# RWKV core: SyncE issues the next pair's vectors ahead of the scatter of the inverses

## What is computed

```python
def step(s, inp):
    r_t, w_t, k_t, v_t, a_t, b_t = inp
    sa = jnp.einsum('dbhvk,dbhk->dbhv', s, a_t)
    s = s * w_t[..., None, :] + sa[..., :, None] * b_t[..., None, :] + v_t[..., :, None] * k_t[..., None, :]
    return s, jnp.einsum('dbhvk,dbhk->dbhv', s, r_t)
```

## Time and profile before

| | |
|---|---|
| median of 3 runs | 3182.29 us (3176.93 to 3184.63) |
| profiled execution | 3185.66 us |
| its span | 3183.8 us |
| TensorE busy | 2941.7 us (92%) |
| VectorE busy | 1476.0 us (46%) |
| ScalarE busy | 684.6 us (22%) |
| GpSimd busy | 1123.4 us (35%) |
| granted clock of TensorE | 0.959 of full speed |

### The profile page before, as it was taken

The page is one execution under the profiler, slowest core; times in us unless marked ns, Lnnn a source line. Parts: engine busy times, 40 slices in busy tenths (PEclk is TensorE's granted clock), DMA queues, the critical chain, the costliest instruction groups (busy, mean ns, idle before and its releaser), DMA issues.

```text
span 3183.8 us, 59340 instructions
## 1 busy us (share of the span) xinstructions
PE 2941.7 (92%) x24772; PEld 2417.9 (76%) x24772; DVE 1476.0 (46%) x1845; ACT 684.6 (22%) x1013; POOL 1123.4 (35%) x663
## 2 busy tenths in 40 slices
PE   6799998899998489988998999999999999999996
PEld 0577886687776488988786888888888888888885
DVE  0676677445866434444425533333333343333336
ACT  0222222102222112122113212122222212122221
POOL 0343343434332112110343444444444444444442
PEclk7899998899999799999999999999999999999998
DMA  9675566532333654444432232232232233223332
GB/s 404 236 242 179 193 221 214 175 83 74 142 110 137 171 112 89 89 94 122 179 99 66 93 96 96 93 96 96 93 96 97 93 97 95 93 95 98 94 95 110
DMA packets 221753, 410.74 MB, mean 129 GB/s; under 512 B 133696, under 2 KB 135488, under 8 KB 214720
## 3 DMA queue, kind: packets, MB, share of 16 engines
q1 hardware_dynamic: 190880, 308.18, 30.9%
q10 hardware_dynamic: 30336, 96.64, 8.8%
q0 software_dynamic: 288, 2.10, 0.2%
HBM read 365.96 MB, written 40.91 MB: 128 GB/s over the span
## 4 chain that ended last, share of the span: by engine, by line
PE 62%; DVE 2%; issue 2%; DMA 0%; ACT 0%; POOL 0%; POOLq 0%; SPq 0%; DVEq 0%; ACTq 0%
PE bank L1075 17%; PE bank L1076 16%; PE bank L1074 16%; PE bank L797 7%; PE bank L813 2%; PE bank L885 1%; PE bank L873 1%; PE bank L959 1%; PE bank L957 1%; DVE buf L1941 0%; DVE buf L1942 0%; PE bank L821 0%; DMA buf<-lnrows 0%; PE bank L834 0%; DVE buf L1898 0%
## 5 line engine op out<-in xcount | busy, mean ns | idle before, releaser
L640 POOL TENSOR_TENSOR buf<-buf 128x1024 fp32r<-128x1024 f32 x288 | 696.6, 2419 | 1023.7 <-ACT buf L1274 1023.7
L1075 PE MATMUL bank<-buf 128*128 128x512 f32 x2304 | 911.2, 395 | 0.0
L1076 PE MATMUL bank<-buf 128*128 128x512 f32 x2304 | 907.4, 394 | 0.0
L1074 PE MATMUL bank<-buf 128*128 128x512 f32 x2304 | 901.3, 391 | 0.6 <-POOL buf L640 0.4
L1274 ACT CAST buf<-buf 128x1024 fp32r<-128x1024 f32 x288 | 302.6, 1051 | 1260.8 <-PE bank L1076 1259.5
L1074 PEld LDWEIGHTS bank<-buf 128*128 128x128 f32 x2304 | 433.1, 188 | 107.1 <-issue 3.2
L1075 PEld LDWEIGHTS bank<-buf 128*128 128x128 f32 x2304 | 432.6, 188 | 100.1 <-issue 0.5
L1076 PEld LDWEIGHTS bank<-buf 128*128 128x128 f32 x2304 | 432.4, 188 | 92.7
L664 PE MATMUL bank<-buf 128*128 128x512 f32 (+1 forms) x1168 | 430.1, 368 | 22.2 <-POOL buf L613 13.0
L665 PE MATMUL bank<-buf 128*128 128x512 f32 (+1 forms) x1168 | 422.6, 362 | 0.0
L666 PE MATMUL bank<-buf 128*128 128x512 f32 (+1 forms) x1168 | 417.1, 357 | 0.0
(11 more groups left out here) (219 smaller groups left out, 2200.6 us busy)
## 6 DMA issues: line engine op xcount, KB each, us to landing
buf<-stream SPq DMA_DIRECT2D x382, 512.0 KB, 3.5
buf<-adarows ACTq DMA_DIRECT2D x108, 512.0 KB, 4.9
buf<-ada SPq DMA_DIRECT2D x32, 1024.0 KB, 13.3
scaled_keys<-buf ACTq DMA_DIRECT2D x18, 768.0 KB, 5.5
buf<-scaled_keys SPq DMA_DIRECT2D x18, 768.0 KB, 6.6
buf<-adarows SPq DMA_DIRECT2D x20, 512.0 KB, 6.5
buf<-inverse_image SPq DMA_DIRECT2D x48, 192.0 KB, 5.2
buf<-tokens SPq DMA_DIRECT2D x4, 1536.0 KB, 21.5
```

Source lines behind the costliest of these rows:

```text
L640: G.tensor_tensor(wl2[b % SPLIT2], raw2[b], wh2[b % SPLIT2].bitcast(F32), ALU.subtract).then_inc(split2, 1)
L1074: pe.matmul(bank[:, :], lh, rh, start=start, stop=False)
L1075: pe.matmul(bank[:, :], lh, rl, start=False, stop=False)
L1076: return pe.matmul(bank[:, :], ll, rh, start=False, stop=stop)
```

## The change

In the loop over pairs 1 to 5, the call that loads the next pair's vectors moves from behind the scatter to ahead of it. No operation, transfer or wait is added or removed. In pairs 1 to 4 the scatter's four issues, and the waits in front of them, now stand behind the wait of the vectors' loads and their four issues; in pair 5 there are no vectors to load.

```diff
             load_receptances(1)
             for j in range(1, BPAIRS):
                 gather(j)
-                scatter(j)
                 if j + 1 < BPAIRS:
                     load_vectors(j + 1)
+                scatter(j)
                 load_inverses(j)
                 if j + 1 < BPAIRS:
                     load_receptances(j + 1)
```

## The result

The changed kernel takes 3199.21 us (median of 20 runs, 3185.0 to 3203.85) against 3182.86 us of the kernel before beside it (20 runs): ratio 1.0048, 95% interval 1.0038 to 1.0057, 16.3 us slower. Its profiled execution took 3199.28 us with a span of 3197.4 us.

A forecast was written before the change was run, and what follows sets the result against it. TensorE was taken to bound the kernel, the change acting through when it leaves the RWKV core. Arrival 9.2, clock 6.3 and later transfers 1.0 summed to +16.5 us: 3182.3 to 3199 us, range 3183 to 3213 (forecast case 3189 to 3212).

The forecast's parts named there:

- The vectors gain nothing: SyncE's queue: the next pair's vector loads wait for their buffers, not the scatter, so issuing them first gains 0.
- V: Time SyncE issues the vectors of pair j+1; claimed set by ScalarE's last front copy and unmoved by the change.
- The arrival of the inverses: Pairs 1 to 4: inverse loads wait for the scatter's landing behind the vectors, delaying TensorE's inverse; +9.2 us (+7.2 to +20).
- the high end of 15.6: Upper bound, in us after the vectors' issue, for the scatter's image being written; 14.8 was taken, low end 14.5.
- TensorE's clock and what follows: TensorE's clock falls after its wait at the inverse, +6.3 us; SyncE's later transfers cause pauses, +1.0 us.
- three longer falls: TensorE at half clock after the wait in three pairs of four, 3 x 2.1 = +6.3 us (0 to +9).
- The 1 us for receptances and late inputs: These loads, issued some 6 us later, run beside TensorE's inverse and bring pauses, 0.25 us a pair, +1 us.
- Cover and pass-through: The gather's substitution ends 17 us and more before the vectors' issue, covering its delay; the core's delay reaches the end in full.
- Side by side: Rival: scatter transfers beside the vectors, not behind them, so inverses land earlier; -14 us, 3168 us, chance 0.08.
- Arrival without the clock: Rival: TensorE arrives shortly before the inverses and its clock holds; +7 us, 3189 us, chance 0.16.
- That nothing happens: Rival: order changes but the wait for the image ends before the inverses matter; 0 us, 3182 us, chance 0.04.
- TensorE's mid-block pauses: Pauses such as 4.02 and 2.93 us before the inverse, at no program wait, during dense DMA traffic; instruction refills left unproved.

The follow-up runs named there:

- e1: Changed kernel without the scatter's four stores in pairs 1 to 4 and without the wait for their landing; 3181.60 us, ratio 1.0003 to the kernel before.
- e8: Order of the kernel before, but SyncE also waits for VectorE's last rc copy of the pair before, between vectors and inverses; 3197.65 us, ratio 1.0053.
- e5: Changed kernel with 60 spare matmuls on TensorE ahead of the wait for the inverses in pairs 1 to 4; 3195.39 us, ratio 1.0033.
- e2: Changed kernel with the scatter of pairs 1 to 4 stored to spare tensors, inverses loaded without waiting for its landing; 3190.01 us, ratio 1.0031.
- e4: Changed kernel reordered: scatter and inverses issued ahead of the next pair's vectors; 3173.61 us against 3180.53 of the kernel before, ratio 0.9982.
- e6: Changed kernel with K and V of the next pair issued behind the inverses, only A and B ahead of the scatter; 3195.10 us, ratio 1.0030.
- e7: Changed kernel reordered, inverses ahead of the next pair's A and B, its K and V only behind the next gather; 3185.78 us, ratio 1.0010.

## Why the prediction was right, point by point

**The time.** Forecast +16.5 us and 3199; measured 16.3 us and 3199.2. The sum is better than its terms: one was too small and another too large by nearly the same; that it fits to 0.2 us is luck.

**The vectors gain nothing.** Right: V follows F by 0.02 us in both kernels, and e1 has the time of before.

**The arrival of the inverses: forecast +9.2 us, measured +12.5.** The mechanism is shown (e1 takes it away, e8 makes it again by another way). Its size was low. The image was awaited until V+14.8, 14.8, 16.4 and 14.7, forecast 14.8; from first inverse load to TensorE's start it took 11.5, 12.5, 11.5 and 12.3 us, forecast 11.5 from the single case of pair 0. Pair 3's late image and two slow loads are the 3.3 us. The loads lie inside the bounds given, and so does the start of each inverse (V+26.3 to V+28.0 in 25.8 to 29.0), but pair 3's image at V+16.4 lies beyond the high end of 15.6; its second store alone took 5.2 us to issue.

**TensorE's clock and what follows: forecast +7.3 us, measured +4.6.** Behind the wait the clock was at its lower level in all four pairs, not three. Windows from the first block on, kernel after, pairs 1 and 4:

```profile
1180.39:1183.40 3.01, 3.01 (x56) 3.01 (x58) 0.50 (x2) 0.59 (x1) 0.00 (x0) 0.50 1.07 328
...
1413.50:1418.90 5.40, 5.40 (x102) 5.40 (x103) 0.50 (x2) 1.17 (x2) 0.00 (x0) 0.50 0.99 254
```

In the four together 266 matmuls took some 53 ns and not 29.5: 266 x 23.5 ns = 6.3 us, as much as I had for three longer falls. The 1 us for receptances and late inputs had the wrong sign: the pauses of 0.25 us and more in R fell from 5.7 to 4.4 us; why, no run was made for. The receptances did move, by 5.3 to 9.3 us, but the next gather, which waits for TensorE's lows, did not move by 6 us as forecast (-2.5 to +3.2). e5 shows that the growth of R is the clock. What is left, 0.4 us, is in the scatter of single executions.

**Cover and pass-through.** Right: the gather's substitution ended 16.4 us and more ahead of V in every pair, and C grew by what I and R grew.

**The rivals.** Side by side is refuted: image at V+14.7 and later, and in e2 even the scatter's issues lasted to V+11.8. That is also what the trace has to say here to the Trainium skill's warning (*DMA: Bandwidth & Descriptors*, "Queues, rings and completion order") that completion need not be first in, first out: in this queue no image was complete before V+14.7. Overtaking there was once, in pair 3, where the first store landed 0.4 us before the last of the vectors; it was of no use. Arrival without the clock did not come: TensorE waited 3.65 to 5.80 us in each pair. That nothing happens is excluded by the interval.

**TensorE's mid-block pauses.** The prediction left open whether they are refills of its instructions; no experiment was made for it, but the kept traces speak for it. The page of the profile lists the queue that brings instructions, here of the kernel before (packets, MB, share of 16 engines):

```profile
q8 instruction: 217, 3.56, 0.5%
```

These are packets of 16 KB, in the core one for every 126 or so of TensorE's matmuls. In pairs 1 to 4 of all eleven traces TensorE has 161 pauses of 0.4 us and more in mid-block, and each ends 1.2 to 1.8 us after such a packet has arrived; of all its matmuls there only some 13% start in that distance. The pause of 4.02 us is one: its packet came in from 1169.46 to 1170.87, and TensorE went on at 1172.49. Most places where TensorE pauses come back in other kernels: behind the 299th and 673rd matmul of pair 1, say, and they lie some 126 matmuls apart. The 20 waits at the inverse's first block end anywhere from 0.9 to 7.7 us after a packet. So the places are fixed by the stream of instructions, and how long TensorE stands there goes with what else the DMA engines carry (e4, e6, e7). That the transfers delay the packets is the plain reading and is not shown by a run of its own.

## What to carry to other kernels

On a queue that is issued in order, ask of each call not only what it waits for but what the next call then inherits: here a store that had been ready for 16 us and more was put behind a wait and 2.7 MB, and a load that needs its landing inherited both. Put first what is ready first (e4), and account every moved transfer in the stretch where it lands as well as in the one it leaves: e6 (against the changed kernel) and e7 (against e4) won 8 and 4 us in one stretch and lost 4.5 and 17 in the next. Split such a loop at a landmark of the critical engine and compare stretch by stretch; that separates a late arrival from a slower clock, which the total can't.

## What was not expected of the hardware

SyncE's issues are themselves held up while much is under way: the second store of a scatter, issued in 0.71 or 0.72 us in pairs 1 to 4 of the kernel before, took 3.72 to 5.21 us right behind the vectors. A wait of 3.65 us on TensorE was enough for the lower clock, 0.50 for 5.4 us after it resumed, while one of 5.80 us was followed by 2.9 us of it, so the loss is not in proportion to the wait. Nor is the length of a pause alone what decides: in the changed kernel a pause of 2.02 us in pair 2 was followed by a granted clock of 0.50, where one of 2.93 us in the kernel before was not the earlier trace rows. And 1.15 MB of transfers beside the inverse's blocks cost TensorE some 3 us of pauses a pair (17.2 against 5.5 us in four, e7 and e4), with no wait of the program there.
